# State space mixer of a hybrid encoder layer on one core: from tokens in partitions to channels in partitions

## The reference

```
proj = rmsnorm(x) @ w_in          # q, k, v, z, xbc, dtf, dtb, ga, gs
xs, B, C = silu(conv5(xbc))       # 16 heads of 64, two groups of 8 heads, state size 64
dt = softplus(dt + bias); acs = cumsum(dt * A) inside chunks of 128 tokens
y_diag = ((C B^T) * exp(acs_i - acs_j) for i >= j) @ (dt * x)      # within a chunk
states = B^T @ (x * dt * exp(acs_end - acs)); h = h * exp(acs_end) + states
y_off = (C @ h_prev) * exp(acs)                                    # from earlier chunks
y = fwd + flip(the same on flipped input) + d_skip * xs
y = y * silu(z); y = y * rsqrt(mean(y*y over each group's 512 channels) + eps) * norm_g
out = x + (sigmoid(ga) * att @ w_attn_out + sigmoid(gs) * y @ w_ssd_out) @ w_out
```

## Time and profile before

| | |
|---|---|
| median of 3 runs | 2073.14 us (2072.48 to 2078.15) |
| the profiled execution | 2081.7 us, its span 2079.2 us |
| PE / DVE / ACT / POOL busy, share of the span | 89% / 47% / 27% / 28% |
| mean granted TensorE clock | 0.946 |
| z stage and what leads to it | 0 to about 165 us |
| rest stage | 357.5 to 650 us |
| states block, scan block | 875.6 to 929.4 us, 929.4 to 1196.9 us |

### The profile page before, as it was taken

How to read it: one execution, slowest core, us unless ns; L and a number is a source line. 1 busy time by engine, 2 the same in 40 slices (tenths; PEclk the granted TensorE clock), 3 DMA queues, 4 the chain that set the end, 5 groups by cost and what they waited for, 6 DMA issues and landing times. The chain is left out here.

```text
span 2079.2 us, 25134 instructions
## 1 busy us (share of the span) xinstructions
PE 1857.7 (89%) x9122; PEld 1453.3 (70%) x9123; DVE 972.1 (47%) x999; ACT 570.8 (27%) x904; POOL 574.0 (28%) x398
## 2 busy tenths in 40 slices
PE   7999998999998998858888799799769997998797
PEld 5877887888885777614555478588658785776586
DVE  4103663110001773276888723621534877740674
ACT  3212222111111663121211211311234443443332
POOL 3002121111112000155555211200015656553530
PEclk9999999999999998978999899899789998999898
DMA  4202223322222102522211143222536776742652
GB/s 172 93 36 80 68 81 119 99 69 91 70 79 88 45 24 76 193 88 79 66 66 66 43 152 131 113 91 71 209 120 207 282 264 247 279 165 82 211 192 92
DMA packets 97708, 249.38 MB, mean 120 GB/s; under 512 B 8803, under 2 KB 42355, under 8 KB 97644
## 3 DMA queue, kind: packets, MB, share of 16 engines
q1 hardware_dynamic: 83724, 197.76, 27.6%
q0 software_dynamic: 8320, 30.43, 4.3%
q10 hardware_dynamic: 5600, 20.32, 2.4%
HBM read 176.37 MB, written 66.86 MB: 117 GB/s over the span
## 5 line engine op out<-in xcount | busy, mean ns | idle before, releaser
L1889 DVE TENSOR_TENSOR ex_wlo<-ex_raw,ex_whi 128x1024 fp32r<-128x1024 f32 x96 | 147.8, 1554 | 0.0
L1885 DVE CAST ex_whi<-ex_raw 128x1024 fp32r<-128x1024 f32 x90 | 88.6, 988 | 99.2 <-DMA ex_raw<-experts 87.7
L2414 PE MATMUL ex_gu<-ex_whi,ex_xh 128*128 x280 | 116.4, 416 | 16.1 <-issue 10.0
L275 PE MATMUL rest_p<-hi_h,whi_in 128*128 128x512 f32 (+1 forms) x480 | 121.2, 361 | 5.3 <-ACTq L696 5.3
L275 PE MATMUL rest_p<-hi_h,wlo_in 128*128 128x512 f32 (+1 forms) x480 | 120.2, 359 | 0.0
L275 PE MATMUL rest_p<-lo_h,whi_in 128*128 128x512 f32 (+1 forms) x480 | 120.2, 359 | 0.0
L2415 PE MATMUL ex_gu<-ex_wlo,ex_xh 128*128 x280 | 112.2, 401 | 0.0
L2416 PE MATMUL ex_gu<-ex_whi,ex_xl 128*128 x280 | 111.9, 400 | 0.0
L732 POOL TENSOR_TENSOR wlo_in<-wraw_in,whi_in 128x1024 fp32r<-128x1024 f32 x18 | 43.2, 2401 | 220.3 <-ACT whi_in L703 220.3
L275 PEld LDWEIGHTS rest_p<-hi_h,whi_in 128*128 128x128 f32 x480 | 80.5, 189 | 20.9 <-POOLq L728 5.6
L1133 DVE TENSOR_SCALAR nsink<-sink 128x8 f32<-128x8 f32 x1 | 0.2, 171 | 199.7 <-DMA sink<-sink 199.7
(11 more groups left out here) (366 smaller groups left out, 4534.8 us busy)
## 6 DMA issues: line engine op xcount, KB each, us to landing
ex_raw<-experts SPq DMA_DIRECT2D x96, 512.0 KB, 6.5
wraw_in<-units SPq DMA_DIRECT2D x36, 512.0 KB, 4.1
y_slots<-ex_y ACTq DMA_DIRECT2D x35, 512.0 KB, 3.9
rest<-rest_out SPq DMA_DIRECT2D x20, 640.0 KB, 5.1
xtok<-conv_tok SPq DMA_DIRECT2D x10, 640.0 KB, 3.3
sst_x<-xtok SPq DMA_DIRECT2D x10, 576.0 KB, 3.7
z_x<-x SPq DMA_DIRECT2D x10, 512.0 KB, 4.2
ztok<-z_out SPq DMA_DIRECT2D x10, 512.0 KB, 2.8
```

The costliest lines, as they stand in the source:

```text
L275: mm = pe.matmul(out[:, n, 0:size], w[:, kk, :], h[:, kk, c:c + size], start=(kk == 0 and w is whi and h is hi), stop=(kk == ktiles - 1 an ...
L1885: eng.tensor_copy(self.hi[:, e % 2, n, :], self.raw[e % 2][:, n, :]).then_inc(self.w_hi[n], 1)
L1889: eng.tensor_tensor(self.lo[:, e % 2, n, :], self.raw[e % 2][:, n, :], self.hi[:, e % 2, n, :].bitcast(F32), ALU.subtract).then_inc(self.w ...
L2414: pe.matmul(gu[s][:, :], xh[s][:, kk, :], hi, start=(kk == 0), stop=False)
```

## The change

The state space part is laid out with channels in the partitions and tokens along the free axis.

- z is made by channel: the weights are stationary, and 2, 4 and 4 token tiles stream (256, 512, 512 columns), stored as `zch`.
- In the rest stage PE also makes two rows per head and direction (the cumulative sum, and ln dt minus it) for all tokens, in four 16-row bands of PSUM; ACT copies them and the exponent of the sum, and they go to DRAM as `frow`, `lrow`, `erow`. Two of the five small sums go.
- The class `States` takes the place of the states block: beside the last tiles of the rest stage it makes the chunk states (8 steps of two chunks), DVE runs the recurrence, and ACT stores them to DRAM.
- The scan works in 20 units (chunk, group). PE adds a one-row-plus-one-row product (K=2) per head and direction, in four row groups, to a mask; ACT takes the exponent; DVE weighs by C B^T once; PE applies with x stationary in column halves and writes 64 channels by 128 tokens. Skip and carried terms accumulate in the same PSUM. The mean of squares is a product with all ones, which leaves it in every partition, so POOL's `pow` and DVE's variance work on 128x128 for each unit. No transpose is left.

```diff
-                pe.matmul(out, k.const[:, C_GT:C_GT + P], rf[quad % 2][:, :, :], start=True, stop=False)
-                pe.matmul(out, k.const[:, C_LT:C_LT + P], rb[quad % 2][:, :, :], start=False, stop=True).then_inc(seg_done, 1)
+                for r in range(4):
+                    pe.matmul(seg[:, r, :], idr[:, :], shut[:, r % 2, :].unsqueeze(1).to_broadcast([P, 4, P]), start=True, stop=False)
+                for c in range(4):
+                    for r in range(4):
+                        rows = slice(32 * r, 32 * r + 2)
+                        mm = pe.matmul(seg[:, r, c * P:(c + 1) * P], ar[s][rows, 4 * g + c, :], br[s][rows, 4 * g + c, :],
+                                       start=False, stop=(c == 3))
...
+            def apply(w):
...
+                for c in range(4):
+                    heads = [2 * (4 * g + c) + par for par in range(2)]
+                    out = [yt[w % 2][par * 64:(par + 1) * 64, c, :] for par in range(2)]
+                    x = [xs[s][:, h * SSD_HEAD:(h + 1) * SSD_HEAD] for h in heads]
+                    for par in range(2):
+                        pe.matmul(out[par], x[par], di[:, heads[par], :], start=True, stop=False)
+                    for n in ways(t):
+                        for par in range(2):
+                            h = heads[par] % HPG
+                            pe.matmul(out[par], hs[s][rows, n, h * SSD_HEAD:(h + 1) * SSD_HEAD], cs[s][rows, n, h, :],
+                                      start=False, stop=False)
+                    pe.wait_ge(m_ready, 4 * w + c + 1)
+                    for n in range(2):
+                        for par in range(2):
+                            mm = pe.matmul(out[par], x[par], mx[(4 * w + c) % 8][:, 2 * par + n, :], start=False, stop=(n == 1))
+                    mm.then_inc(m_used, 1)
+
+            def mean(w):
...
+                for c in range(4):
+                    mm = pe.matmul(ms[:, 0:P], k.const[:, C_ONE:C_ONE + P], sq[w % 2][:, c, :], start=(c == 0),
+                                   stop=(c == 3))
...
+        def _(pool):
...
+            for w in range(UNITS):
+                pool.wait_ge(var_done, w + 1)
+                if w >= 2:
+
+                    pool.wait_ge(normed, w - 1)
+                pool.tensor_tensor(rs[w % 2][:, :], var[w % 2][:, :], nh[:, :], ALU.pow).then_inc(rstd, 1)
...
+        def _(dve):
...
+            for w in range(UNITS + 3):
+                if 1 <= w <= UNITS:
+                    gate(w - 1)
+                if 2 <= w <= UNITS + 1:
+                    variance(w - 2)
+                if w >= 3:
+                    rest(w - 3)
+                if w + 1 < UNITS:
+                    weigh(w + 1, 0)
+                    weigh(w + 1, 1)
+                if 2 <= w <= UNITS + 1:
+                    norm(w - 2)
+                if w + 1 < UNITS:
+                    weigh(w + 1, 2)
+                    weigh(w + 1, 3)
+                if w // 2 + 1 < NT:
+                    carried_c(w // 2 + 1, w % 2)
...
+        for t in range(t0, t0 + m):
+            c = slice((t - t0) * P, (t - t0 + 1) * P)
+            out = [self.sums[n % 2][32 * j:32 * j + 16, c] for j in range(4)]
+            fwd, bwd = slice(0, 16), slice(16, 32)
+            pe.matmul(out[0], q.dta[:, t, fwd], up, start=True, stop=True)
+            pe.matmul(out[1], q.dta[:, t, bwd], down, start=True, stop=True)
+            pe.matmul(out[2], q.ln_dt[:, t, fwd], ident, start=True, stop=False)
+            pe.matmul(out[3], q.ln_dt[:, t, bwd], ident, start=True, stop=False)
+            pe.matmul(out[2], q.minus[:, t, fwd], up, start=False, stop=True)
+            mm = pe.matmul(out[3], q.minus[:, t, bwd], down, start=False, stop=True)
...
+    def tensor(self, pe, s):
+        pe.wait_ge(self.scaled, s + 1)
...
+        for n in range(2):
+            x = self.x[n][s % 2]
+            for g in range(2):
+                mm = pe.matmul(self.sums[n][g * 64:(g + 1) * 64, :], x[:, D + g * 64:D + (g + 1) * 64],
+                               self.xd[n][:, g * 512:(g + 1) * 512], start=True, stop=True)
...
+            for c in range(8, n_tiles):
+                product(c, c % 2)
+                if FIRST <= c < FIRST + states.STEPS:
+                    states.tensor(pe, c - FIRST)
...
+    GROUPS = ((0, 2), (2, 4), (6, 4))
...
+            def product(n):
+                g, ct = TILES[n]
+                t0, m = GROUPS[g]
+                pe.wait_ge(lo_s, t0 + m)
...
+                    pe.matmul(out, w.hi[u][:, col], hi[:, kk, tok], start=(kk == 0), stop=False)
+                    pe.matmul(out, w.hi[u][:, col], lo[:, kk, tok], start=False, stop=False)
+                    mm = pe.matmul(out, w.lo[u][:, col], hi[:, kk, tok], start=False, stop=(kk == KT - 1))
...
-    stage_ssd_states(k, q)
```

More of the change, by code:

```diff
@@ L684, in _ @@
             tables.sync_tables(sp)
[L685 to L689 removed]
+            for c in range(n_tiles):
+                if c + 4 < n_tiles:
+                    load(c + 4, c % 2)
+                if c == FIRST - 2:
+                    sp.wait_ge(states.free, 1)
+                    sp.wait_ge(decays.rows_stored, 96)
+                    states.load(sp, 0)
+                    states.load(sp, 1)
+                if FIRST <= c < FIRST + states.STEPS - 2:
+                    states.load(sp, c - FIRST + 2)
                 store(c, c % 2)
@@ L744, in _ @@
             decays.vector(dve)
-            tables.vector(dve)
+            tables.vector(dve, states.free)
+            states.scale(dve, 0)
+            for s in range(states.STEPS):
+                states.carry(dve, s)
+                if s + 1 < states.STEPS:
+                    states.scale(dve, s + 1)
         @block.tensor
@@ L878, in _ @@
             norm.root(pool, 1)
-            for n in range(1, 8, 2):
-                w.split_lo(pool, n)
-            for t in range(2, NT):
+            w.split_lo(pool, 1)
+            w.split_lo(pool, 3)
+            norm.root(pool, 2)
+            w.split_lo(pool, 5)
+            w.split_lo(pool, 7)
+            for t in range(3, NT):
                 norm.root(pool, t)
@@ new lines, in _ @@
+            for c in range(4):
+                exp(0, c)
+                if c == 0:
+                    cb_copy(0)
+            for w in range(UNITS + 2):
+                for c in range(4):
+                    if w + 1 < UNITS:
+                        exp(w + 1, c)
+                        if c == 0:
+                            cb_copy(w + 1)
+                    if c == 1 and 1 <= w <= UNITS:
+                        square(w - 1)
+                if w >= 2:
+                    split(w - 2)
@@ new lines, in variance, with norm @@
+            def variance(w):
+                dve.wait_ge(ms_done, w + 1)
+                if w >= 2:
+                    dve.wait_ge(rstd, w - 1)
+                dve.tensor_scalar(var[w % 2][:, :], ms[:, 0:P], 1.0 / 512, EPS, ALU.mult, ALU.add).then_inc(var_done, 1)
+            def norm(w):
+                g = w % 2
+                dve.wait_ge(rstd, w + 1)
+                if w >= 2:
+                    dve.wait_ge(lo_done, w - 1)
+                for c in range(4):
+                    ins = dve.scalar_tensor_tensor(out=v[w % 2][:, c, :], in0=u[w % 2][:, c, :],
+                                                   scalar=gain[:, 4 * g + c:4 * g + c + 1], in1=rs[w % 2][:, :],
+                                                   op0=ALU.mult, op1=ALU.mult)
+                ins.then_inc(normed, 1)
```

856 lines of the change are left out of this document (389 added, 467 removed).

## The result

The changed kernel takes **2355.51 us** (median of 4 runs, 2353.36 to 2357.52). The kernel before took 2072.81 us beside it (4 runs, 2069.85 to 2078.15). The ratio is 1.1371, 95% interval 1.1335 to 1.1406: 13.7% slower. The forecast was 2325 with a range up to 2350, so the sign and the power's part were right and the time lies 5.5 us above the range. The profiled execution took 2353.36 us, span 2351.6; before it was 2081.7 and 2079.2, so the spans differ by 272.4 us.

What follows compares the result with a forecast made beforehand. It took POOL's 128-column `pow` plus DVE's own work to bound the scan's turn; z +4, rest stage +20 and states with scan +228 made +252, 2081.7 to 2334, less 8.6: 2325 us, range 1990 to 2350 (likeliest case 2275 to 2350).

Steps and rivals of the forecast that it cites:

- the rest stage's +20: Rest stage: chunk states +14.2, row sums +6, two small sums -0.3; DVE, ACT and row transfers hidden; +20 us.
- the 8.6 us taken off at the end: Whole kernel: the profiled execution before lay 8.6 us above the median, so 2334 became 2325 us.
- The power: Scan: POOL's `pow` on 128 columns costs 0.39 + 128 x 0.149 = 19.5 us; true cost between 0.65 and 19.5.
- DVE's share: Scan: DVE's own work per unit, gate, variance, rest, weighings, norm, carried factor and handing over, 6.6 us.
- The first rival: Scan: `pow` is cheap per column, PE's 9 us a unit binds, down to 1992 us; chance 0.30.
- The turn: Scan: weighings and rest come behind `pow`, not under it, so a turn is 6.6 + 19.5 = 26.0 us.
- Its own sign: Scan: DVE's weighings would show a maximum near 20 us, beside DVE's wait for `pow`.
- The aside that without exclusion 41 us would hide: Scan: without the exclusion rule three DVE instructions, 2.05 us a turn, would hide under `pow`, 41 us in all.
- The scan block: Scan: twenty turns 521 less 8, 35 before and 1.5 behind, 549 us; +228 against the two blocks' 321.3.
- States 8 x 1.78: Rest stage: eight steps of chunk state products on PE at 1.78 us each, +14.2 us.
- Row sums 6: Rest stage: PE's row sums in four overlapping 16-row bands take 6 us, ends 5 and 16.
- The z stage: Start: 256- and 512-column matmuls cost 112.3 for 110.4 us, first product 2 to 5 later; +4, between 0 and +8.

Runs made afterwards that it cites:

- experiment 6: Root on ACT, POOL making tiles 4 and 5's low weight parts before the line's transfers: 1984.07 us; besides, chunk state products in the first step only: 1969.61 us.
- experiment 2: Changed kernel with POOL's power on 64 columns only, 16 columns only, or partitions 0 to 31 only: 2152.50, 2007.90 and 2362.44 us.
- pow_mult: Changed kernel with POOL's power replaced by a multiplication of the same operands, the norm's root left out: 2009.11 us, ratio 0.9666 to the kernel before.
- norm_later: Changed kernel with DVE's norm one turn later, behind the weighings, gated tile and root three deep: 2257.92 us, ratio 1.0849 to the kernel before.
- root_act: Changed kernel with the root made on ACT as exp(-0.5 ln v) instead of POOL's power: 2007.28 us, ratio 0.9684 to the kernel before.

## Why the prediction was right or wrong

**What failed.** The time lies above the range. The step that failed is the rest stage's +20, which put PE's wait for POOL behind the moved line product at nothing (8.3 us, experiment 6; the stage took +30), and with it the 8.6 us taken off at the end, though the profiled execution of the changed kernel did not lie above its median. The power was right as a mechanism and 1.3 us too small each time, 25 us, but an error of 23 us in DVE's share made up for most of it, and that is luck. The terms one by one:

**The power, right.** The step that decided, 19.5 us from two rows of one and two columns, measured 20.77. The slope was 7% too small, 1.3 us in each of 20 turns, 25 us. To go by these two rows was right for the reason given, that the second column was not cheaper than the first; experiment 2 shows the line. But 19.5 was called the upper end of the true cost, and it was none. The first rival (cheap power) was wrong in its premise; what it forecast for a cheap power, 1992 us, `pow_mult` gave as 2009.

**The turn, about right in size and wrong in its parts.** "A turn is then 6.6 + 19.5 = 26.0 us", since weighings and rest "come behind `pow`, not under it". It was 26.74, but rest and two weighings ran first and the power waited for them at its start, 1.58 us; the other 4.39 us are DVE's queue between two powers, since the next variance stands behind the norm that waits for this power. Both pictures add up DVE's whole work and the power, and no total can tell them apart. `norm_later` can: where the power shut DVE out for its whole time the turn would have stayed at 26, and it fell to 20.74. What failed here is the sentence that made a rule for a power out of a weighing that stood still beside a multiplication. Its own sign, weighings with a maximum near 20 us, didn't appear (sources of the changed kernel, DVE):

```profile
L1815 DVE TENSOR_TENSOR scan_m<-scan_m,scan_cb x80: 679/683/692, 931.4 to 1398.3; 128x512 f32<-128x512 f32 x80
```

It cost no time in this forecast. The aside that without exclusion 41 us would hide was wrong with it: in the order as it stands the power waits for those three instructions, and `norm_later` hid 100 us of DVE's queue by an edit that the forecast didn't look for.

The Trainium skill, SBUF — State Buffer, "Who interferes with whom", has the two engines' instructions exclude one another for the whole instruction. For a multiplication on POOL the trace agrees; for the power it does not: in 20.76 us of power in `norm_later` carried factor, rest and four weighings of DVE took what they take alone. Something of it shows only at the power's start, as 0.2 us for DVE or as the wait for DVE's row.

**The scan block, right by luck.** It was to take 549 us and took 553.2; states and scan +232, forecast +228. The parts: 35.0 us to the first power (35 forecast); 515.4 from its start to the end of the last (951.31 to 1466.67), where 521 - 8 = 513 were put down; 2.8 behind it (1.5). In the 515.4 the powers are 25 us more than forecast and all that DVE adds is 100 instead of 123. A full turn adds 5.97 with the carried factor and 4.84 without, where the forecast had 6.6 on average: it added up durations, but a 0.68 us instruction's successor starts 0.60 us after it (1109.28 to 1109.88). The 35.0 is itself of this one profile. In that of `norm_later` the first power came 43.0 us into the block; the granted clock of the first 44 us was 0.58 there and 0.79 here.

**The rest stage, +20 forecast, +30 measured: a size and a missed wait.** States 8 x 1.78 = 14.2 were 8 x 2.09 = 16.7. Row sums 6 were 4.3: four bands start within 20 ns of one another, and the next token tile's 0.43 us later, so the four did overlap (timeline of PE):

```profile
397.78 0.28 PE L625 MATMUL rest_spare<-const,ssd_dta 128*16 128x128 f32 x1
...
397.79 0.28 PE L626 MATMUL rest_spare<-const,ssd_dta 128*16 128x128 f32 x1
...
397.80 0.28 PE L627 MATMUL rest_spare<-const,ssd_ln_dt 128*16 128x128 f32 x1
...
397.80 0.28 PE L628 MATMUL rest_spare<-const,ssd_ln_dt 128*16 128x128 f32 x1
```

Another 8.3 is the wait of experiment 6; in the nine kernels that keep the old order on POOL it is 6.7 us in every trace, and it is in neither of the two that change it. The working looked at SP's queue for the moved step and not at POOL's, though the line product's release passes through DVE to POOL. About 1 us of the stage has no name, and neither have the 2 us between this stage and the scan.

**The z stage, +4 forecast, +8.1 measured**, just past the end of its range. The first product starts at 23.34 us instead of 18.96, behind two token tiles, +4.4:

```profile
23.34 0.58 PE L1097 MATMUL z_p<-hi_h,z_hi 128*128 128x256 f32 x1 [3.53 <-DVE lo_h L1131]
23.72 0.41 PE L1098 MATMUL z_p<-lo_h,z_hi 128*128 128x256 f32 x1
23.93 0.41 PE L1099 MATMUL z_p<-hi_h,z_lo 128*128 128x256 f32 x1
```

The first 256-column products then start 0.21 us apart at the lower clock, where 0.125 was put down; from 26.65 us on it is 0.12, as forecast. From 38 to 46 us the granted clock is 0.65 where it was 1.00 before; in the 8 us ahead of that PE was busy for 4.52 us, before for 5.89. What the forecast let "the longer work per weight unit" give back wasn't given back. This is read from the trace; no experiment was made on it.

**The last subtraction.** 8.6 us were taken off because the profiled execution of before lay that far above its median. The profiled execution of the changed kernel lay 2.2 below its own. That step was worth 11 of the 30 us by which the forecast was low, beside 10 in the rest stage, 4 in the z stage, 4 in states and scan and 2 between them. The range's upper end had carried it along, and none of its cases had a missed wait or a power above 19.5; its two terms, row sums in series (+10) and z at +8 (+4), give 2339 and not 2350.

## What to carry to other kernels

Read an operation's cost per column off the trace's two smallest shapes before widening it, and ask which axis it goes by: here each of 128 columns held one value, the same in every partition, and was paid at 160 ns. Then look for an engine that does the same with a table. When a total comes out as a sum of two engines' work, ask whether they exclude one another or only stand in one another's queue, since the second can be undone by moving a step; and for each moved step follow its release to the last engine that waits for it.

## What the runs showed of the hardware that I had not expected

- POOL's element-wise power takes 0.35 us and 159.6 ns a column (from 16, 64 and 128 columns, 2.90, 10.55 and 20.77 us), with 32 partitions as with 128. A multiplication of the same 128 columns took 0.456 us at its least (`pow_mult`), 45 times less.
- A power on POOL doesn't get started while DVE's row of two-operand instructions goes on without a gap (it takes 0.38 us more with one in the row, 1.58 with three, 2.79 with nine), but a row that starts 0.06 us behind the power loses only 0.2 us and then runs beside it (`norm_later`).
- ACT makes the same root in two instructions of 0.31 us (`root_act`).
- Two-row products in four row groups pass at 37 ns an instruction of 128 columns (32 in 1.17 us, granted clock 1.00).
